# Neighbourhood attention by tiles of 8 rows by 16 columns, each query tile against two of four shifted key blocks

## The reference, cut to what matters

```python
def one_row(r):                                   # B, H, rows = 8, GRID_W = 64, kh = 8, kw = 16
    rs = jnp.clip(r - kh // 2, 0, rows - kh)      # always 0: all eight rows are in the window
    kb = ...kg[rows rs..rs+kh][:, :, :, col_idx]  # col_idx[c] = the 16 columns from clip(c - 8, 0, 48)
    s_loc = einsum('bhcd,bhicjd->bhcij', qr, kb) * scale + bias     # bias: learned, by row and column offset
    s_ctx = einsum('bhcd,bhnd->bhcn', qr, k_ctx) * scale            # all 256 context keys
    p = softmax(concat([s_loc, s_ctx]))
    return p_loc @ vb + p_ctx @ v_ctx
```

## Time and profile before

| | |
|---|---|
| median of 3 runs | 2558.0 us (2555.36 to 2560.51) |
| span of the profiled execution | 2555.3 us |
| neighbourhood attention, layer 0 | 305.5 to 484.5 us of the span |
| neighbourhood attention, layer 1 | 1665.8 to 1775.5 us of the span |
| mean granted TensorE clock | 0.990 |

### The profile page before, as it was taken

The page is one execution under the profiler, slowest core; times in us unless marked ns, Lnnn a source line. Parts: engine busy times, 40 slices in busy tenths (PEclk is TensorE's granted clock), DMA queues, the critical chain, the costliest instruction groups (busy, mean ns, idle before and its releaser), DMA issues. The chain is left out here.

```text
span 2555.3 us, 40630 instructions
## 1 busy us (share of the span) xinstructions
PE 2413.2 (94%) x17330; PEld 1522.9 (60%) x17330; DVE 1040.0 (41%) x2260; ACT 669.6 (26%) x1371; POOL 115.7 (5%) x167
## 2 busy tenths in 40 slices
PE   4999999999999899999999999998999999989897
PEld 3898877778687445343444688876777643333232
DVE  4545455344775423222222554454458421112113
ACT  3622232322543212121111462143335311010101
POOL 1000100000000101000000000100000000000000
PEclk9999999999999999999999999999999999999999
DMA  6111466121551999999999412321227389999996
GB/s 224 53 53 37 123 206 199 66 97 48 182 204 56 368 416 408 409 408 408 403 401 396 134 59 67 83 84 61 95 72 234 144 338 421 420 420 420 420 421 278
DMA packets 198725, 596.46 MB, mean 233 GB/s; under 512 B 12006, under 2 KB 120784, under 8 KB 150032
## 3 DMA queue, kind: packets, MB, share of 16 engines
q1 hardware_dynamic: 186400, 556.51, 56.3%
q0 software_dynamic: 12144, 37.34, 4.9%
HBM read 561.23 MB, written 32.57 MB: 232 GB/s over the span
## 5 line engine op out<-in xcount | busy, mean ns | idle before, releaser
L1115 PE MATMUL ps<-h_hi,m_lo 128*128 128x512 f32 (+1 forms) x1152 | 344.8, 371 | 2.1 <-DVE arena L2327 1.7
L1562 PE MATMUL ps<-arena 128*32 128x512 f32 x1740 | 257.2, 593 | 1.3 <-DVE arena L2589 1.3
L1563 PE MATMUL ps<-arena 128*32 128x512 f32 x588 | 256.6, 593 | 0.0
L1115 PEld LDWEIGHTS ps<-h_hi,m_lo 128*128 128x128 f32 x1152 | 207.0, 189 | 49.6 <-issue 11.1
L1088 PE MATMUL ps<-m_lo,h_hi 128*128 128x256 f32 (+1 forms) x1248 | 230.8, 287 | 5.2 <-DVE m_lo L2298 3.3
L1115 PE MATMUL ps<-h_lo,m_lo 128*128 128x512 f32 (+1 forms) x576 | 204.0, 354 | 0.0
L1088 PEld LDWEIGHTS ps<-m_lo,h_hi 128*128 128x128 f32 x1248 | 194.0, 193 | 13.7 <-issue 10.0
L1676 PE MATMUL ps<-arena 128*64 128x512 f32 x720 | 168.4, 611 | 18.4 <-DMA arena<-in_moe_w_up 17.1
L1088 PE MATMUL ps<-m_lo,h_lo 128*128 128x256 f32 (+1 forms) x624 | 176.1, 282 | 0.0
L1562 PEld LDWEIGHTS ps<-arena 128*32 128x32 f32 x1740 | 71.6, 110 | 164.4 <-issue 163.2
L1088 PE MATMUL ps<-h_hi,m_lo 128*128 128x512 f32 (+1 forms) x512 | 141.8, 354 | 7.9 <-DVE h_lo L2422 6.9
(11 more groups left out here) (413 smaller groups left out, 4542.3 us busy)
## 6 DMA issues: line engine op xcount, KB each, us to landing
arena<-in_moe_w_up SPq DMA_DIRECT2D x94, 1024.0 KB, 17.3
arena<-in_moe_w_gate SPq DMA_DIRECT2D x93, 1024.0 KB, 19.5
arena<-in_moe_w_down SPq DMA_DIRECT2D x92, 1024.0 KB, 17.8
ring<-in_w_in SPq DMA_DIRECT2D x42, 1024.0 KB, 5.3
arena<-in_ada_w SPq DMA_DIRECT2D x34, 1024.0 KB, 5.5
oT<-in_moe_w_down SPq DMA_DIRECT2D x25, 1024.0 KB
oT<-in_moe_w_up SPq DMA_DIRECT2D x24, 1024.0 KB
oT<-in_moe_w_gate SPq DMA_DIRECT2D x16, 1024.0 KB
```

The lines of the kernel that those rows point to most:

```text
L1115: last = mm(to, w[:, k, cols], h[:, k, seg], start=n == 0 and k == 0, stop=n == 2 and k == KD - 1)
L1562: mm(up_banks(j)[r][32 * b:32 * b + 32, :], c_xg[:, k, j, 32 * b:32 * b + 32], w, start=k == 0, stop=k == KD - 1)
L1563: last = mm(up_banks(j)[r][96:128, :], c_xg[:, k, j, 32 * r:32 * r + 32], up[:, kk, 512:1024], start=k == 0, stop=k == KD - 1)
```

## The change

The latent tokens of branch A are taken in another order. A query tile is now all 8 rows of 16 columns: tile `t` has columns 16t to 16t+15. The keys and values are cut into four blocks of 8 rows by 16 columns, which are shifted by 8 columns: block `b` (1 to 3) has columns 16b-8 to 16b+7, and block 0 has columns 0 to 7 and 56 to 63. Every query tile then needs only two blocks (`NA_BLOCKS`), so 256 latent keys in place of 512.

- The copies of the projected queries and keys write their tiles in this order (`placed`). For queries it is one instruction as before, for keys two.
- The values are stored to device memory in row order (a new DMA) and loaded back as blocks by five DMAs on GpSimd's queue, behind the eight bias loads and ahead of the weight loads of branch B. They count up `mla_in`, and TensorE waits for it at the first latent pair of `attention(l, 0)`.
- Scores: 256 near keys and 256 context keys share one PSUM bank. VectorE adds the bias (zeros over the context half) to all 512, negated, and takes the minimum in one instruction; ScalarE takes one exponential of 512 with one sum.
- Two transposes of latent pieces a unit in place of four, a copy of 256 columns in place of 512, four key tiles a pair in place of six.
- The bias has three tables (first tile, middle tiles, last tile). It is built by one memset and eight additions with inner runs of 16 or 8 elements, in place of four additions. Each of the eight loads now has 512 pieces of 128 B, where it had 896 pieces of 256 B.
- The finished tile is written back in row order.

Branch B and the context units keep their instructions. The core of the diff:

```diff
+NA_ROWS, NA_COLS = SEQ // GRID_W, 16
+NA_TILES = GRID_W // NA_COLS
+NA_BLOCKS = ((0, 1), (1, 2), (2, 3), (0, 3))
+NA_SHIFTS = ((8, 16), (0, 16), (8, 0))
+
+
+def block_columns(b):
+
+    return list(range(NA_COLS * b - 8, NA_COLS * b + 8)) if b else list(range(0, 8)) + list(range(GRID_W - 8, GRID_W))
...
-        bias = carve(ar, 18, H, 14, 64)
-        bias_raw = carve(ar, 32, H, 14, 64)
+        bias = carve(ar, 18, 1 + 3 * H, 256)
+        bias_raw = carve(ar, 32, NA_ROWS, H, 32)
...
+        def placed(job, src):
+
+            m, _, _, _, where, dst, _ = job
+            if where is not LAT or m not in (7, 8):
+                return [(dst, src)]
+            if m == 7:
+                return [(dst.rearrange("p (t r c) -> p r t c", t=NA_TILES, c=NA_COLS), src.rearrange("p (r t c) -> p r t c", t=NA_TILES, c=NA_COLS))]
+            inner = src.rearrange("p (r w) -> p r w", w=GRID_W)[:, :, 8:GRID_W - 8].rearrange("p r (s c) -> p r s c", c=NA_COLS)
+            edges = src.rearrange("p (r o c) -> p r o c", o=8, c=8)[:, :, 0:8:7, :]
+            return [(dst[:, P:].rearrange("p (s r c) -> p r s c", r=NA_ROWS, c=NA_COLS), inner),
+                    (dst[:, 0:P].rearrange("p (o r c) -> p r o c", o=2, c=8), edges)]
...
+        def near_blocks(cols, t):
+
+            a, b = NA_BLOCKS[t - CT]
+            return cols.rearrange("p (b n) -> p b n", n=P)[:, a:b + 1:b - a, :]
+
+        def attended(i, t):
+
+            return CT if t < CT else CT + 2 if i == 0 else NT
...
-                pool.dma_start(rpb_in[0:H * 15, :], a["na_rpb"][l].rearrange("h r c -> (h r) c")).then_inc(rpb_landed, 16)
+                pool.dma_start(rpb_in[0:H * 15, :], a["na_rpb"][l].rearrange("h r c -> r h c")).then_inc(rpb_landed, 16)
                 pool.wait_ge(rpb_padded, before("rpb_padded", l) + 1)
                 pool.dma_start(rpb_scratch[l], rpb_pad[0:H * 15, :]).then_inc(rpb_flat, 16)
                 pool.wait_ge(rpb_flat, before("rpb_flat", l) + 16)
+                jobs_done(pool, l, "nav")
+                pool.dma_start(nav_scratch[l].rearrange("(t p) d -> p t d", p=P), nav[:, CT:NT, :]).then_inc(rpb_flat, 16)
                 pool.wait_ge(goT_ok, before("goT_ok", l) + NQ[l])
-                for half in range(2):
-                    for h in range(H):
-                        src = bass.AP(rpb_scratch[l].tensor, (h * 15 + 1 - half) * PADW, [[1, 64], [PADW, 14], [1, 64]])
-                        pool.dma_start(bias_raw[64 * half:64 * half + 64, h, :, :], src).then_inc(bias_in, 16)
+                for r in range(NA_ROWS):
+                    src = bass.AP(rpb_scratch[l].tensor, (7 - r) * H * PADW + 40, [[1, NA_COLS], [PADW, NA_ROWS * H], [1, 32]])
+                    pool.dma_start(bias_raw[NA_COLS * r:NA_COLS * r + NA_COLS, :, :, :].rearrange("p a h b -> p (a h) b"), src).then_inc(bias_in, 16)
+                pool.wait_ge(rpb_flat, before("rpb_flat", l + 1))
+                by_row = nav_scratch[l].rearrange("(r w) d -> r w d", w=GRID_W)
+                for b in range(1, NA_TILES):
+                    pool.dma_start(nav[:, CT + b, :], by_row[:, NA_COLS * b - 8:NA_COLS * b + 8, :]).then_inc(mla_in, 16)
+                for o in range(2):
+                    pool.dma_start(nav[64 * o:64 * o + 64, CT, :], by_row[:, 56 * o:56 * o + 8, :]).then_inc(mla_in, 16)
                 pool.dma_start(w_uq, a["mla_w_uq"][l].rearrange("(k p) n -> p k n", p=P)).then_inc(mla_in, 16)
                 pool.dma_start(w_ukv, a["mla_w_ukv"][l]).then_inc(mla_in, 16)
...
-                            mm(ps[2 * e][:, :], q, kk[:, LAT], start=True, stop=True)
+                            mm(ps[2 * e][:, CTX:2 * CTX].rearrange("p (a b) -> p a b", b=P), q, near_blocks(kk[:, LAT], t), start=True, stop=True)
                     for e, (q, kk) in enumerate(operands):
-                        mm(ps[2 * e + 1][:, 0:CTX], q, kk[:, CX], start=True, stop=True).then_inc(s_up, 1)
+                        mm(ps[2 * e + (t < CT)][:, 0:CTX], q, kk[:, CX], start=True, stop=True).then_inc(s_up, 1)
...
-                        for t in range(CT, NT):
+                        for t in range(CT, attended(i, us[u][1])):
...
+                        if i == 0 and t == CT:
+                            pe.wait_ge(mla_in, before("mla_in", l + 1))
                         pe.wait_ge(p_act, before("p_act", idx) + lats[2 * p + 1])
                     pe.wait_ge(p_dve, before("p_dve", idx) + 2 * p + 2)
-                    keys = range(NT if t >= CT else CT)
+                    keys = range(attended(i, t))
                     for kt in keys:
                         for e in range(2):
                             h = us[2 * p + e][0]
-                            v = nav[:, kt, 64 * h:64 * h + 64] if i == 0 else mv[:, kt, h, :]
+                            at = CT + NA_BLOCKS[t - CT][kt - CT] if kt >= CT and i == 0 else kt
+                            v = nav[:, at, 64 * h:64 * h + 64] if i == 0 else mv[:, kt, h, :]
...
-                    do(dst, bank[0:m, 0:size], ACT.Copy, scale=scale).then_inc(proj_act, 1)
+                    for to, src in placed(projections(l)[name][i], bank[0:m, 0:size]):
+                        last = do(to, src, ACT.Copy, scale=scale)
+                    last.then_inc(proj_act, 1)
...
+                    if t >= CT and i == 0:
+                        do(prob[:, u % 2, 0:SEQ], s_bias[:, u % 2, :], ACT.Exp, scale=-1.0, bias=st[:, c + 2:c + 3], accum_out=st[:, c + 4:c + 5]).then_inc(s_exp, 1)
+                        return
                     if t >= CT:
-                        src = s_bias[:, u % 2, :] if i == 0 else ps[2 * (u % 2)][:, :]
-                        do(prob[:, u % 2, LAT], src, ACT.Exp, bias=st[:, c + 2:c + 3], accum_out=st[:, c + 3:c + 4])
+                        do(prob[:, u % 2, LAT], ps[2 * (u % 2)][:, :], ACT.Exp, bias=st[:, c + 2:c + 3], accum_out=st[:, c + 3:c + 4])
...
-                    do(probT[:, u % 2, CT:NT, :].rearrange("p a b -> p (a b)"), ps[4][:, :], ACT.Copy).then_inc(p_act, 1)
+                    last = attended(i, us[u][1])
+                    do(probT[:, u % 2, CT:last, :].rearrange("p a b -> p (a b)"), ps[4][:, 0:P * (last - CT)], ACT.Copy).then_inc(p_act, 1)
...
-                        r = 6 - 2 * (t - CT)
-                        v.tensor_tensor_reduce(s_bias[:, u % 2, :], lat[:, :], bias[:, h, r:r + 8, :].rearrange("p a b -> p (a b)"),
-                                               1.0, NEG, ALU.add, ALU.max, st[:, c:c + 1])
-                    else:
-                        v.reduce_max(st[:, c:c + 1], lat[:, :], AX_X)
+                        at = 1 + H * ((t > CT) + (t == NT - 1)) + h
+                        v.tensor_tensor_reduce(s_bias[:, u % 2, :].rearrange("p (a b) -> p a b", a=2), lat[:, :].rearrange("p (a b) -> p a b", a=2),
+                                               bias[:, 0:at + 1:at, :], -1.0, -NEG, ALU.add, ALU.min, st[:, c + 2:c + 3]).then_inc(s_max, 1)
+                        return
+                    v.reduce_max(st[:, c:c + 1], lat[:, :], AX_X)
                     link(v.reduce_max(st[:, c + 1:c + 2], cx[:, 0:CTX], AX_X))
...
-                    if us[u][1] >= CT:
+                    if us[u][1] >= CT and i:
...
-                    link(v.tensor_copy(to, ps[5][:, 256:384]))
-                    v.tensor_tensor(to, to, ps[5][:, 384:512], ALU.mult).then_inc(o_ok, 1)
+                    o, sums = ps[5][:, 256:384], ps[5][:, 384:512]
+                    if i == 0 and t >= CT:
+                        to = na_oT[:, h // 2, LAT].rearrange("p (r w) -> p r w", w=GRID_W)[:, :, NA_COLS * (t - CT):NA_COLS * (t - CT) + NA_COLS]
+                        o, sums = [x.rearrange("p (r c) -> p r c", c=NA_COLS) for x in (o, sums)]
+                    link(v.tensor_copy(to, o))
+                    v.tensor_tensor(to, to, sums, ALU.mult).then_inc(o_ok, 1)
...
-                for h in range(H):
-                    last = v.tensor_tensor(bias[:, h, :, :], bias_raw[:, h, :, ::-1],
-                                           window.unsqueeze(1).to_broadcast([P, 14, 64]), ALU.add)
+                v.memset(bias[:, 0, :], 0.0)
+                for table, shifts in enumerate(NA_SHIFTS):
+                    for n, kk in enumerate(shifts):
+                        edge = NA_BLOCKS[(0, 1, NA_TILES - 1)[table]][n] == 0
+                        width, parts = (8, 2) if edge else (NA_COLS, 1)
+                        for o in range(parts):
+                            at = P * n + 64 * o
+                            to = bias[:, 1 + H * table:1 + H * table + H, at:at + P // parts].rearrange("p h (r c) -> p r h c", c=width)
+                            inside = window[:, 2 * table + n, 8 * o:8 * o + width].unsqueeze(1).unsqueeze(1).to_broadcast([P, NA_ROWS, H, width])
+                            end = 32 - kk - 8 * o
+                            last = v.tensor_tensor(to, bias_raw[:, :, :, end - width:end][:, :, :, ::-1], inside, ALU.add)
                 link(last)
                 if l == 0:
```

26 lines of the change are left out of this document (16 added, 10 removed).

## The result

The changed kernel takes 2536.0 us (median of 4 runs, 2534.2 to 2537.2) where the kernel before takes 2558.4 us (4 runs). The ratio is 0.9912, with a 95% interval of 0.9900 to 0.9924, that is 22.4 us less (19.4 to 25.6). The forecast was 2536.5 us, 21.5 us less. The total was right to within a microsecond.

What follows compares the result with a forecast made beforehand. The prediction took TensorE, busy 94% of the span, to bound the kernel. It summed 20.2 (TensorE) + 1.9 (waits, clock) - 0.6 (copies) = 21.5 us, so 2558.0 - 21.5 = 2536.5 us, range 2529 to 2548.

Steps and rivals of the forecast that it cites:

- What bounds the kernel: Both attention stages: TensorE's instruction issue sets the pace; VectorE and ScalarE have a third to a half free.
- Scores, values, transposes, 20.2 us: TensorE, 16 latent pairs: 0.43, 0.45 and 0.38 us saved a pair, 20.2 us in all, ends 18.5 to 21.5.
- The chains, 1.9 us: VectorE and ScalarE in latent units: fewer instructions shorten TensorE's waits, mainly 1.4 us at layer 1's second pair's scores.
- On its own it buys nothing: Latent units: 0.73 us less on VectorE and 0.64 on ScalarE gain only what they take off TensorE's waits.
- The clock, +0.3 us: Layer 1's last values: clock averages 0.60, so the eight dropped records save an estimated 0.3 us extra.
- Copies, -0.6 us: Keys' copy split in two, twice a layer: 4 x 0.15 us lost, counted in full; hidden they cost nothing.
- Bias, queue, DMA sharing, nothing each: Bias 4.3 us against 4.1, GpSimd loads with 27 us of cover, DMA sharing with 4.9 us: no cost.
- The surcharge at 1.5 times: Bias additions in short runs at 1.5 times the time: 7 us, 3 us more; not charged, kept as the end.
- Rival 1: Short-run patterns are dear in bias, `normalise` and copies: gain only 13.9 us, 2544 us; chance 0.10.
- Rival 2: Shorter chains close most of layer 1's 8.2 us of idle time: gain 27 us, 2531 us; chance 0.03.
- Rival 3: VectorE sets a unit's pace, so TensorE's saved time comes back as waits: 2558 us; chance 0.03.
- Rival 4: Values land late at the first latent pair: one us for each past 27, slower once 48 us late; chance 0.02.

Runs made afterwards that it cites:

- a4_chains: Changed kernel with only VectorE's and ScalarE's shorter chains undone (separate maxima, joining, two exponentials, sums added) in latent units: ratio 0.9942 to the kernel before.
- b2_bias_twice: Changed kernel with the additions that build the bias made twice, 4.4 us more of VectorE ahead of each stage: ratio 0.9954 to the kernel before.
- b4_filled: Changed kernel with unread identity transposes (10, 26 and 6) in TensorE's idle time at the end of layer 1's attention: ratio 0.9893 to the kernel before.
- d1_order: Changed kernel with VectorE's gate-product copy and low-part halves moved later at the end of layer 1's attention stage: ratio 0.9890 to the kernel before.
- e1_all_undone: Changed kernel with TensorE's three parts and the VectorE and ScalarE chains undone, new layout, bias, copies and loads kept: ratio 0.9996 to the kernel before.
- b1_tensor_all: Changed kernel with TensorE's three parts undone together (512 score columns, six key tiles, four transposes), shorter chains kept: ratio 0.9984 to the kernel before.

## Why the prediction was right, and which terms were not

*What bounds the kernel.* Right. Undoing TensorE's parts costs 18.5 us of 22.1.

*Scores, values, transposes, 20.2 us.* The steps have the durations forecast (0.54 us for 0.53, 0.92 for 0.91, and 0.14 or 0.22 a unit for 0.14 to 0.2). What they are worth is 18.5 us (stages) or 18.4 us (ratio), at the lower end of 18.5 to 21.5; worked out again from its own terms, that end is 17.9. The forecast counted every shortened step in full. In layer 0 that was nearly so, 9.7 of 10.1; in layer 1 8.8 of 10.1, since part of the saving went into waits for VectorE: TensorE's idle time there is 5.2 us with the long steps and 7.0 or 7.6 us with the short ones. For that the forecast had charged only 0.2 us.

*The chains, 1.9 us.* This is the term that was mis-sized: 3.6 us with TensorE's work as before, 6.4 us in the changed kernel. The forecast looked at waits that stand in the trace of before, and the wait at the second pair's scores did shrink (1.5 to 0.4 or 1.0 us, 0.5 to 1.1 us for 1.4 forecast). It left out the waits that would have opened as TensorE got faster, had VectorE not become faster with it: the `normalise` waits, 4.0 us with the long chain and 2.2 with the short one. "On its own it buys nothing" was wrong.

*The clock, +0.3 us.* It was counted at one place only. The last values took 2.3 us before and 0.9 or 1.2 us after, 1.1 to 1.4 us less where 0.45 + 0.3 was forecast; how much of that is the change is open, as 16 records took 1.73 us in a4_chains and b2_bias_twice. The stretch behind the stage, which was at 1.00 in the profile before, lay in the low clock and took 2.8 to 3.2 us; b4_filled and d1_order give them back. The forecast cut its window at the stage's end, and that is where this loss begins. Against e1_all_undone, which has the waits of the kernel before, the stretch is only 1.8 to 2.2 us longer, so part of the loss is where the low clock happened to fall.

*Copies, -0.6 us.* Hidden. The keys' copy on ScalarE became two of 0.49 and 0.27 us where it was 0.60, the 0.15 us forecast. But the time from branch C's first transpose (L1241 before, L1286 after), ahead of these copies, to layer 0's stage is 187.9 us and was 188.0, and in layer 1 it is 155.7 us in both.

*Bias, queue, DMA sharing, nothing each.* Right. The bias takes 4.3 us for 4.3, with some luck: its own rate and starts (1084 ns for 896 elements with 0.15 us of start) give 4.4 us for the additions without the memset. The surcharge at 1.5 times would by the same rows have been some 2.5 us and not 3. The cover of the weight loads is 33 us for 27, since they were issued 19 us ahead of the stage and not 16, and land 4.1 us after issue and not 8.7. ScalarE's wait for the chunk behind them shrank from 4.2 to 2.4 us.

*The sum.* In place of 20.2 + 1.9 - 0.6 = 21.5 us the runs give 18.5 + 3.6 = 22.1 for the stages (the profiles show 22.2 and 23.2), nothing for the copies, and -2 to -3 for the clock behind layer 1's stage. That is 19 to 20 us. The last 2 to 3 us of the 22.4 are not accounted for: the ratio's interval reaches down to 19.4 us, and single stretches outside the stages differ by 1 to 5 us from profile to profile. A forecast that was right by compensation, and in part by luck, is no proof of its terms. The range's lower end was added up wrongly as well: 21.5, 3.5 and 2.6 us below 2558.0 is 2530.4, not 2529.

*The rivals.* Rival 1 fell on the 685 ns row. Rival 2 fell too: TensorE's idle time in layer 1's stage went from 7.9 us to 7.0 and 7.6, so the waits did not close; the chains were worth more than counted because they kept others from opening. Rival 3 fell with b1_tensor_all. Rival 4's mechanism was there when the queue was made 48 us longer, and not before. But its price left out layer 0. At one us for each us past the cover, 47.8 - 33 = 14.8 us, the kernel would have stayed 7 us faster than the one before. It was 12 us slower, as the gate products' stores of layer 0 stood behind the same transfers and made its stage 14.9 us longer.

## What to carry to other kernels

Price a shorter chain on a side engine in the timeline as it will be after the main engine's steps have shrunk, not in the one of before: waits that do not exist yet are what it prevents. Undo each side alone and both together; where the singles add up to more than the pair (24.9 to 22.1 us here), the sides share a wait. And look past the end of the stage that is shortened: here the dense stretch behind a thin one took 1.0 to 3.4 us more at the low clock in every version that kept the waits ahead of it, save in the one profile of the kernel before, and moving 3 us of VectorE's work behind the last thing that TensorE waits for was worth 5 us.

## What the runs showed of the hardware

- A stretch of 4.5 us with TensorE busy for 0.83 us was followed by the low clock in the changed kernel, and one of 4.8 us with 0.91 us busy in the kernel before. There the window of 3.7 us over the last values has 0.54 and the one behind it 1.00; in the changed kernel 8.5 us behind the values have 0.50, which is 1.2 GHz. With 2.4 us of wait less there was none.
- Where the low clock falls differs between profiles whose steps and waits at that place are the same: the 14 transposes behind the stage took 1.75 us in the kernel before and 3.25 us in e1_all_undone, and the last 16 value records 0.90 us in the changed kernel and 1.73 us in b2_bias_twice.
- 4.4 us more of VectorE's work at the start of a stage cost 6.9 us in layer 1, where a wait of 4.0 us ended at the low clock (0.72 in its window).
- Eight loads of 64 KB each landed 3.4 us after issue and were issued every 0.63 us, where eight of 224 KB took 6.1 and 0.78 us. The weight loads behind them landed in 4.1 us and not 8.7.
- A hundred transfers of 256 bytes held GpSimd's queue for 0.48 us each. In the same stretch two weight chunks of 1 MB on SyncE's queue landed 7.8 us after issue (median) and not 5.3.
